# Router logits taken from transposed, un-normalised residual sums; second token tile's norm moved to ScalarE and GpSimd; weight splits moved beside the last expert

## The chip, the cores and the metric

The kernel runs on one core of one Trainium2 chip. The metric is device time in microseconds. Three runs of the kernel before gave a median of 1345.87 us (1345.45 to 1346.3). About 0.2% (2.7 us) is what a measurement of this kernel can tell from no change.

## The reference, cut to what matters

256 tokens of width 1024 pass two layers of a first block and one layer of a second block. In each of the first two layers a mixer (retention in layer 0, sparse attention "nsa" in layer 1) is followed by a layer norm, a mixture of 16 experts and another layer norm:

```python
h = layer_norm(ALPHA * h + mix, ln_mix_g[l], ln_mix_b[l])
h = layer_norm(ALPHA * h + moe(h, router_w, router_b, gate[l], up[l], down[l]), ln_ffn_g[l], ln_ffn_b[l])

# moe: x is the normed h
aff = sigmoid(x @ router_w)                 # 16 scores a token
sel = aff + router_b                        # best group of 4, then the best 2 experts in it
w = aff * chosen; w = w / w.sum(-1)
for e in range(16):
    y += w[:, e:e+1] * ((silu(x @ w_gate[e]) * (x @ w_up[e])) @ w_down[e])
```

With s the residual sum before the norm, mu its mean and r its inverse deviation, the logits of the normed x are r * (s @ (g * W)) - r * mu * sum(g * W) + sum(b * W); g and b are the norm's gain and shift, W the router's weights.

## The kernel before, in words

Each engine has its own instruction stream, written out in the order in which it runs: PE (TensorE), DVE (VectorE), ACT (ScalarE), POOL (GpSimd), and SP (SyncE), which issues nearly all transfers in order on one queue. They meet only at semaphores. Tokens come in two tiles of 128, `tt` = 0 and 1. `X` holds the residual stream, tokens on partitions.

Dense linears: weights come in blocks of 512 x 512 f32 (1 MB) into a ring `raw` of 7. ACT copies a block to fp32r `whi` (`split_hi`, L489), DVE subtracts to `wlo` (`split_lo`, L499), PE multiplies three products. Two blocks (`AHEAD`) of the next linear are split ahead of it. Activations are split likewise: PE transposes `X` (L742), ACT writes `th` (L749), DVE writes `tl` (L757).

Around a router (`out_and_norm_*`, L1062 on, then `moe_layer_*`, L2715 on): PE makes the output linear tile by tile (L615). DVE adds ALPHA * X + product (`residual_half`, L1051), takes statistics, and norms `X` in place (`centre_half` L810, `shift_half` L814), with the root on ACT. Only then PE transposes the normed tile, ACT and DVE split it, PE makes the logits (L1103, L1108), DVE reduces them (L1140), ACT takes the sigmoid (L1131), and DVE ranks experts in some 40 small instructions up to L1183. PE meanwhile puts ALPHA * X into PSUM with 8 matmuls on `ident_a` (L1113), counted by `rows_summed`. Then come slot numbers (L1122 to L1127), one-hot `pick` tiles (L1212), and the gather of each expert's tokens from `xn_h`/`xn_l`, the split copy of `X` (L1379).

Experts (`paired_*`, L1310 on): 96 blocks of 1 MB go through 20 homes. Sixteen homes come free before or during the output linear and are filled early. Home 16 (`rows`) is the memory of `X` itself: SP waits at L1323/L1324 for `xn_l_done` and `rows_summed` before it issues, and all later issues of the queue stand behind it. Every later block waits for the use of the block 20 before it. After block 95 SP issues the two rows of the next norm (`gb`, L1342), and then the next linear's `raw` blocks. For the last expert, 15, the order on ACT is: transposed hidden (L1502), `y(14)` (L1495), `y(15)`, then the two `split_hi` of the next linear (L2743), then the table of the root (L2744). DVE makes the low half of `y` (L1539) behind ACT's, PE scatters it to the rows (L1442), and DVE norms tile 0, then tile 1 (L3084 on). The two `split_lo` stand between: before the low half of the transposed tile 0, and behind tile 1's norm.

Of the kernel before, what the change touches and what calls it, by code (L numbers as in the profile page):

```python
# [53 lines left out]
C_ID, C_ROW, C_BEFORE, C_ONES, C_COL, C_I16, C_I4, C_FOLD, C_END = 0, 128, 448, 576, 580, 584, 600, 604, 668  # L54
# [45 lines left out]
def block_program(nc, a, out):  # L100
    with ExitStack() as ctx:
# [41 lines left out]
        ident_a, pre_gT = small[:, 128:256], small[:, 64:64 + DC]  # L143
        rw = keep("rw", [P, DC, E], F32)
# [4 lines left out]
        class Arena:  # L149
# [15 lines left out]
        fold = cst[:, C_FOLD:C_FOLD + SLOTS]  # L165
# [12 lines left out]
        ang = A("ang", [P, 4, TT, 96], at=gb_at + 4096 + 1024)  # L178
        ret_sd = A("ret_sd", [P, 2, 3, P], at=gb_at)
# [130 lines left out]
        cmp_loaded, cmp_turned, cmp_copied, cmp_built = (  # L310
            sem(n) for n in ("cmp_loaded", "cmp_turned", "cmp_copied", "cmp_built"))
# [13 lines left out]
        x_late, conv_loaded, conv_turned, conv_taken = (  # L325
            sem(n) for n in ("x_late", "conv_loaded", "conv_turned", "conv_taken"))
# [101 lines left out]
        halved = [l_ret_out, l_nsa_out, l_b_out, l_mix, l_down]  # L428
        two_piece = [l_up.b0 + 20, l_up.b0 + 21]
# [78 lines left out]
        def linear_sync(sp, l, between=None):  # L508

            def body(j, turn):  # L510
                for kb, kc in enumerate(l.groups):
                    if between is not None:
# [549 lines left out]
        def out_and_norm_tensor(pe, l, xh, xl, layer, c0=0, opened=False, low=same, ready=None):  # L1062

            def first_half(tt, n):
                if tt == 1 and n == 1:
                    half_turn_tensor(pe, 1 + 2 * layer, tokens(X), normed_by(pe, 4 * layer), (0,))
            halves_tensor(pe, l, xh, xl, in_order, c0, opened, None, first_half, low, ready)

        def out_and_norm_scalar(act, l, layer):
# [3 lines left out]
            early_table(ACT.Sqrt)  # L1073
            root_half(act, 4 * layer, 0)
            half_turn_scalar(act, 1 + 2 * layer, 0)
            nc.scalar.activation(straight(xn_h, 0), neighbours(X, 0), ACT.Copy).then_inc(xn_h_done, 1)
            root_half(act, 4 * layer, 1)

        def out_and_norm_vector(dve, st, o, l, layer):

            for i in (2, 3):
                split_lo(dve, sweep_first, l.b0 + i, 0)
            residual_half(dve, o, l, 0, 0)
# [9 lines left out]
        def router_tensor_logits(pe, k, layer):  # L1093
            for tt in range(TT):
                if tt == 1:
                    half_turn_tensor(pe, k, tokens(X), normed_by(pe, 4 * layer), (1,))
                at = 2 * E * tt
                if tt == 0:
                    pe.wait_ge(half_lo, 4 * k + 2)
                for half in range(2):  # L1100
                    pe.wait_ge(half_hi, 4 * k + 2 * tt + half + 1)
                    for c in range(4 * half, 4 * half + 4):
                        nc.tensor.matmul(PS[:, 4, at:at + 2 * E], th[:, c, tt * P:(tt + 1) * P],  # L1103
                                         rwx[:, c].rearrange("p a e -> p (a e)"), start=(c == 0), stop=False,
                                         skip_group_check=True)
                    pe.wait_ge(half_lo, 4 * k + 2 * tt + half + 1)
                    for c in range(4 * half, 4 * half + 4):
                        last = nc.tensor.matmul(PS[:, 4, at:at + E], tl[:, c, tt * P:(tt + 1) * P], rwx[:, c, 0, :],  # L1108
                                                start=False, stop=(c == DC - 1), skip_group_check=True)
            last.then_inc(to_vector, 1)  # L1110
            for tt in range(TT):
                for half in range(2):
                    last = nc.tensor.matmul(PS[:, 2 * tt + half, :], ident_a[:, :], X[:, tt, half * BW:(half + 1) * BW],  # L1113
                                            start=True, stop=False, skip_group_check=True)
            last.then_inc(rows_summed, 1)

        def router_tensor(pe, st, k, layer):

            router_tensor_logits(pe, k, layer)
# [9 lines left out]
        def router_scalar(act, st):  # L1129
            inbox(act, st)  # L1130
            nc.scalar.activation(affinity, score, ACT.Sigmoid).then_inc(to_vector, 1)  # L1131
# [353 lines left out]
        def paired_scalar(act, s, layer):  # L1485
# [22 lines left out]
            for e in range(E):  # L1508
# [8 lines left out]
                if e >= 1:  # L1517
                    y(e - 1)
# [1819 lines left out]
```

## Time and profile before

| | us |
|---|---|
| median of three runs | 1345.87 |
| the profiled execution, its own time | 1347.77 |
| its span (first to last instruction) | 1345.6 |
| PE busy | 1279.1 (95%) |
| DVE busy | 737.5 (55%) |
| ACT busy | 539.2 (40%) |
| GpSimd busy | 74.9 (6%) |
| queue of SP (q1), share of 16 transfer engines | 66.0% |

The span is what the engines' instructions cover; 2.2 us of the execution lie outside it. The busy share of PE is an average over stages: it says nothing of a stage in which PE waits for DVE or for a transfer. A stage is read from the instructions in order of time and from what ended their idle time.

### The profile page before, as it was taken

Reading aid. Unit: us, or ns where it says so; the run is one execution under the profiler, and the core shown is the slowest. Engines: PE = TensorE matmul, PEld = TensorE weight load, DVE = VectorE, ACT = ScalarE, POOL = GpSimd, SP = SyncE. Lnnn points to the kernel's source line nnn. Section 1 sums busy time; section 2 is a strip of 40 time slices with the busy share of each in tenths; the row PEclk is TensorE's granted clock in tenths of the full one; section 3 lists DMA queues with packets and bytes.
Section 4 is the critical chain, followed back from the end, with each engine's and each line's share of the span. In section 5 each row is a group of like instructions: output and inputs, shape, how many; then the busy total and the mean of one; then the engine's idle time right before and its main releaser. Section 6 shows DMA issues by size and latency. Waiting matters only on the chain.

```text
span 1345.6 us, 16658 instructions
## 1 busy us (share of the span) xinstructions
PE 1279.1 (95%) x6652; PEld 893.4 (66%) x6652; DVE 737.5 (55%) x1231; ACT 539.2 (40%) x787; POOL 74.9 (6%) x78
## 2 busy tenths in 40 slices
PE   7999998999999799998999999799999998899998
PEld 5887887444443487676444443477888877899986
DVE  4766657233232685886233222675674566578772
ACT  4445442111121433682111111456546644465551
POOL 0000000000000000000000000006760000000000
PEclk9999998999999899898999999799999989899999
DMA  9654487999999655317999999664454426355540
GB/s 344 205 182 131 157 330 309 418 422 421 421 422 415 222 194 210 141 62 291 401 421 421 422 421 418 228 200 154 154 161 158 149 96 205 127 185 188 188 156 32
DMA packets 103890, 342.51 MB, mean 255 GB/s; under 512 B 10188, under 2 KB 17020, under 8 KB 79100
## 3 DMA queue, kind: packets, MB, share of 16 engines
q1 hardware_dynamic: 100992, 336.30, 66.0%
q10 hardware_dynamic: 2812, 5.04, 1.1%
q8 instruction: 57, 0.93, 0.3%
q14 instruction: 29, 0.24, 0.0%
HBM read 340.27 MB, written 1.05 MB: 254 GB/s over the span
## 4 chain that ended last, share of the span: by engine, by line
PE 87%; DVE 8%; ACT 3%; issue 1%; DMA 0%; ACTq 0%; DVEq 0%; SPq 0%
PE PS L690 23%; PE PS L1397 16%; PE PS L537 10%; PE PS L1431 9%; PE PS L615 7%; PE PS L593 5%; PE PS L674 2%; PE PS L1379 2%; PE PS L1442 2%; PE PS L742 1%; PE PS L2089 1%; DVE wlo L502 1%; PE PS L1816 1%; ACT whi L496 1%; PE PS L1842 1%
## 5 line engine op out<-in xcount | busy, mean ns | idle before, releaser
L502 DVE TENSOR_TENSOR wlo<-raw,whi 128x2048 fp32r<-128x2048 f32 (+1 forms) x122 | 272.7, 2255 | 101.7 <-ACT whi L496 97.2
L496 ACT ACTIVATE whi<-raw 128x2048 fp32r<-128x2048 f32 (+1 forms) x122 | 224.8, 1876 | 21.3 <-PE PS L593 13.9
L690 PE MATMUL PS<-whi,th 128*128 128x512 f32 x480 | 191.0, 398 | 1.6 <-ACT a_proj L2962 1.5
L690 PE MATMUL PS<-whi,tl 128*128 128x512 f32 x480 | 187.3, 390 | 0.0
L690 PE MATMUL PS<-wlo,th 128*128 128x512 f32 x480 | 186.9, 389 | 0.0
L1397 PE MATMUL PS<-moe_ring,xg 128*64 128x512 f32 x640 | 142.0, 593 | 2.6 <-DVE slot_sum L1555 2.6
L1397 PEld LDWEIGHTS PS<-moe_ring,xg 128*64 128x64 f32 x640 | 46.5, 137 | 91.6 <-issue 91.6
L1569 DVE TENSOR_TENSOR hidden<-hidden,PS 64x256 f32<-64x256 f32 x32 | 13.5, 423 | 170.0 <-ACT hidden L1512 170.0
L690 PEld LDWEIGHTS PS<-whi,th 128*128 128x128 f32 x480 | 90.2, 188 | 21.8 <-ACT a_proj L2962 1.9
L690 PEld LDWEIGHTS PS<-whi,tl 128*128 128x128 f32 x480 | 90.1, 188 | 19.1
L690 PEld LDWEIGHTS PS<-wlo,th 128*128 128x128 f32 x480 | 90.3, 188 | 17.6
L537 PE MATMUL PS<-th,whi 128*128 128x256 f32 x352 | 100.6, 286 | 1.4 <-DVE tl L757 1.4
L537 PE MATMUL PS<-th,wlo 128*128 128x256 f32 x352 | 100.4, 285 | 0.0
L537 PE MATMUL PS<-tl,whi 128*128 128x256 f32 x352 | 100.3, 285 | 0.0
L1539 DVE SCALAR_TENSOR_TENSOR y_split<-PS,w_slot,y_split 64x512 fp32r<-64x512 f32 x60 | 45.0, 749 | 93.7 <-ACT y_split L1495 92.8
L1512 ACT ACTIVATE hidden<-PS 64x512 f32<-64x512 f32 x32 | 18.9, 590 | 183.2 <-PE PS L1397 183.2
L1495 ACT ACTIVATE y_split<-PS,w_slot 64x512 fp32r<-64x512 f32 x60 | 40.9, 682 | 97.1 <-PE PS L1431 96.4
L1431 PE MATMUL PS<-moe_ring,hT 128*64 128x512 f32 x320 | 72.6, 598 | 0.0
L537 PEld LDWEIGHTS PS<-th,whi 128*128 128x128 f32 x352 | 68.4, 194 | 1.8 <-DVE tl L757 1.8
L537 PEld LDWEIGHTS PS<-th,wlo 128*128 128x128 f32 x352 | 68.4, 194 | 0.0
L537 PEld LDWEIGHTS PS<-tl,whi 128*128 128x128 f32 x352 | 68.4, 194 | 0.0
L879 POOL TENSOR_TENSOR rope_t<-b_proj,trig 128x256 f32<-128x256 f32 x48 | 41.5, 896 | 308.3 <-issue 295.3
(425 smaller groups left out, 2080.7 us busy)
## 6 DMA issues: line engine op xcount, KB each, us to landing
moe_ring<-in_moe_w_gate SPq DMA_DIRECT2D x40, 1024.0 KB, 14.1
moe_ring<-in_moe_w_up SPq DMA_DIRECT2D x40, 1024.0 KB, 16.2
moe_ring<-in_moe_w_down SPq DMA_DIRECT2D x40, 1024.0 KB, 19.8
raw<-in_w_in SPq DMA_DIRECT2D x32, 1024.0 KB, 5.2
raw<-in_ret_w_in SPq DMA_DIRECT2D x24, 1024.0 KB, 5.1
raw<-in_w_up SPq DMA_DIRECT2D x20, 1024.0 KB, 5.1
raw<-in_w_down SPq DMA_DIRECT2D x10, 1024.0 KB, 5.0
raw<-in_ret_w_out SPq DMA_DIRECT2D x8, 1024.0 KB, 4.9
```

The lines of the kernel that those rows point to most:

```text
L496: nc.scalar.activation(s.whi[:, high, 0:kc, 0:wide], s.raw[:, slot, 0:kc, 0:wide], ACT.Copy).then_inc(s.hi_done, 1)
L502: nc.vector.tensor_tensor(s.wlo[:, slot, 0:kc, 0:wide], s.raw[:, slot, 0:kc, 0:wide], s.whi[:, high, 0:kc, 0:wide], ALU.subtract).then_inc ...
L537: last = nc.tensor.matmul(PS[:, 2 * p + m // 2, (m % 2) * SEQ:(m % 2 + 1) * SEQ], w[:, k, c, m * P:(m + 1) * P], x[:, c0 + c, :],  start=( ...
L593: last = nc.tensor.matmul(PS[:, bank(j, tt), :], x[:, at, tt * P:(tt + 1) * P], w[:, k, c, :], start=(kb == 0 and c == 0 and i == 0), stop ...
L615: last = nc.tensor.matmul(PS[:, bank(j, tt), :], x[:, at, tt * P:(tt + 1) * P], w[:, k, c, :], start=(not opened and kb == 0 and c == 0 an ...
L674: last = nc.tensor.matmul(PS[:, 2 * (l.n0 % 2) + tt, :], x[:, KC * kb + c, tt * P:(tt + 1) * P], w[:, k, c, :], start=(kb == 0 and c == 0 ...
L690: last = nc.tensor.matmul(PS[:, 2 * (col % 2) + tt, 0:wide], x[:, KC * kb + c, tt * P:(tt + 1) * P], w[:, k, c, 0:wide], start=(kb == 0 an ...
L879: o(nc.gpsimd.tensor_tensor(t[i], u, v, ALU.mult))
L1397: m = nc.tensor.matmul(PS[64 * k:64 * k + 64, gate_up_bank(e), :], x, moe_place(layer, n)[:, c, :], start=(half == 0 and c == 0), stop=(ha ...
L1431: m = nc.tensor.matmul(PS[64 * half:64 * half + 64, down_bank_of(e), :], hT_of(e)[:, 2 * b + c, :], moe_place(layer, down_at(e) + b)[:, 2 ...
L1495: nc.scalar.activation(y_of(e)[rows, half, :], PS[rows, down_bank_of(e), :], ACT.Identity, scale=w_slot[rows, e:e + 1]).then_inc(s.y_hi, 1)
L1539: nc.vector.scalar_tensor_tensor(y_of(e)[low, half, :], PS[rows, down_bank_of(e), :], w_slot[rows, e:e + 1], y_of(e)[rows, half, :], ALU.m ...
```

## The change

What it does:

- Router: PE transposes the residual sums of a tile, not the normed rows, and multiplies them by `rwx`, now the split of g * W. `score_vector` (three DVE instructions a tile) applies mean and inverse deviation; the sigmoid takes scale -1. The constants sum(g*W), sum(b*W) of both layers are made once, during the first linear.
- `norm_half` of tile 0 waits on DVE for the transposes of its sums, because it writes over `X`.
- Tile 1 is normed by ACT (scale and bias) and GpSimd (gain, shift, two halves), GpSimd also makes half of its `xn_l`, DVE the other half, behind the first `pick`.
- Of the four ALPHA * X products of PE, one waits for tile 1's norm ahead of the slot-number matmuls, and the last, which counts `rows_summed`, stands behind the first four gathers.
- End of the experts: SP issues the next linear's first two blocks ahead of the norm's rows; ACT and DVE split them before `y(14)`; DVE takes tile 1's statistics ahead of the low half of tile 0; the next linear opens after the first half of tile 0.

```diff
         def opened_by(pe, k, turn=None):
             def opening(step):
                 if step == 0:
+                    pe.wait_ge(half_lo, 4 * k + 1)
+                if step == 1:
+                    if turn is not None:
+                        turn()
                     pe.wait_ge(half_lo, 4 * k + 2)
-                if step == 1 and turn is not None:
-                    turn()
...
+            def beside_out(tt, n):                      # out_and_norm_tensor
+                if tt == 1 and n == 0:
+                    for half in range(2):
+                        sums_turn_tensor(pe, l, 0, half)
+                if tt == 1 and n == 2:
+                    sums_turn_tensor(pe, l, 1, 0)
+                    for half in range(2):
+                        logits_tensor(pe, k, 0, half)
...
             root_half(act, 4 * layer, 0)                # out_and_norm_scalar
-            half_turn_scalar(act, 1 + 2 * layer, 0)
+            half_turn_scalar(act, k, 0)
+            act.wait_ge(normed, 4 * layer + 1)
             nc.scalar.activation(straight(xn_h, 0), neighbours(X, 0), ACT.Copy).then_inc(xn_h_done, 1)
+            half_turn_scalar(act, k, 1, (0,))
+            half_turn_scalar(act, k, 1, (1,))
             root_half(act, 4 * layer, 1)
...
             residual_half(dve, o, l, 0, 1)              # out_and_norm_vector
             dve.wait_ge(params_in, 16 * st.params)
+            dve.wait_ge(half_turned, 4 * k + 2)
             norm_half(dve, o, 4 * layer, 0)
             residual_half(dve, o, l, 1, 0)
-            half_turn_vector(dve, 1 + 2 * layer, 0)
+            half_turn_vector(dve, k, 0)
+            half_turn_vector(dve, k, 1, (0,))
+            inbox(dve, st)
+            score_vector(o, layer, 0)
             residual_half(dve, o, l, 1, 1)
-            norm_half(dve, o, 4 * layer, 1)
+            half_turn_vector(dve, k, 1, (1,))
+            dve.wait_ge(norm_root, RET_H + 4 * layer + 2)
+            o.then(nc.vector.reciprocal(small[:, 9:10], small[:, 9:10]))
+            o.then(nc.vector.scalar_tensor_tensor(small[:, 10:11], small[:, 2:3], -1.0, small[:, 9:10], ALU.mult,
+                                                  ALU.mult))
+            hand(dve, inverse_done)
...
+        def router_tensor(pe, st, l, layer):
+            k = 1 + 2 * layer
+            logits_tensor(pe, k, 1, 0)
+            sums_turn_tensor(pe, l, 1, 1)
+            logits_tensor(pe, k, 1, 1)
+            residual_tensor(pe, layer, 0, 0)
+            residual_tensor(pe, layer, 0, 1)
+            residual_tensor(pe, layer, 1, 0)            # each: pe.wait_ge(normed, 4 * layer + tt + 1), one matmul
             inbox(pe, st)
...
             selection(paired, 0, layer, rt2, 1)         # router_vector
+            dve.wait_ge(xn_h_done, 3 * layer + 3)
+            dve.wait_ge(xn_l_done, 3 * layer + 2)
+            nc.vector.tensor_tensor(straight(xn_l, 1)[:, 1], neighbours(X, 1)[:, 1], straight(xn_h, 1)[:, 1],
+                                    ALU.subtract).then_inc(xn_l_done, 1)
...
                 elif kind == "rows":                    # paired_sync
-                    sp.wait_ge(xn_l_done, 2 * (layer + 1))
+                    sp.wait_ge(xn_l_done, 3 * (layer + 1))
                     sp.wait_ge(rows_summed, layer + 1)
...
+            linear_sync(sp, behind_experts[layer], last=AHEAD)
             sp.wait_ge(moe_used, MOE_BLOCKS * layer + moe_last(moe_homes.index(("gains", 0))) + 1)
...
-            pe.wait_ge(xn_l_done, 2 * (layer + 1))      # paired_tensor
             for j in range(PER):
+                pe.wait_ge(xn_l_done, 3 * layer + 2 + j // 2)
                 if j == 3:
                     pe.wait_ge(s.xg_first, 2 * layer + 1)
                 gather(0, j, first_bank(j))
+            residual_tensor(pe, layer, 1, 1).then_inc(rows_summed, 1)
...
                 turned(e)                               # paired_scalar; paired_vector alike with split_lo
+                if e == E - 1:
+                    for b in range(AHEAD):
+                        split_hi(act, sweep_first, moe_b0[layer] + b, 0)
                 if e >= 1:
                     y(e - 1)
...
             early_table(ACT.Sigmoid)                    # moe_layer_scalar
-            half_turn_scalar(act, k, 1)
+            act.wait_ge(inverse_done, layer + 1)
+            act.wait_ge(half_turned, 4 * (1 + 2 * layer) + 4)
+            scaled_half(0)
+            router_scalar(act, st)
+            scaled_half(1)
             for h in range(2):
+                act.wait_ge(half_normed, 2 * layer + h + 1)
                 nc.scalar.activation(straight(xn_h, 1)[:, h], neighbours(X, 1)[:, h],
                                      ACT.Copy).then_inc(xn_h_done, 1)
-            router_scalar(act, st)
...
+                rows = [(slice(None), 1, slice(h * BW, (h + 1) * BW)) for h in range(2)]        # gpsimd
+                for h in range(2):
+                    pool.wait_ge(scaled_done, 2 * layer + h + 1)
+                    o.then(nc.gpsimd.tensor_tensor(X[rows[h]], X[rows[h]], gb[:, 0, h * BW:(h + 1) * BW], ALU.mult))
+                    nc.gpsimd.tensor_tensor(X[rows[h]], X[rows[h]], gb[:, 1, h * BW:(h + 1) * BW],
+                                            ALU.add).then_inc(half_normed, 1)
+                pool.wait_ge(half_normed, 2 * (layer + 1))
+                pool.drain().then_inc(normed, 1)
+                pool.wait_ge(xn_h_done, 3 * layer + 2)
+                nc.gpsimd.tensor_tensor(straight(xn_l, 1)[:, 0], neighbours(X, 1)[:, 0], straight(xn_h, 1)[:, 0],
+                                        ALU.subtract).then_inc(xn_l_done, 1)
...
             experts_norm_half(dve, o, 2, 0)             # behind the experts; alike in layer 1
-            split_lo(dve, sweep_first, l_nsa_kv.b0, 0)
+            experts_half(dve, st, o, 1, 0)
             half_turn_vector(dve, 2, 0)
-            experts_half(dve, st, o, 1, 0)
             experts_norm_half(dve, o, 2, 1)
-            split_lo(dve, sweep_first, l_nsa_kv.b0 + 1, 0)
```

In the first linear four transfers of 1024 single floats each (the norms' gains and shifts, one channel a partition) follow the other constants, DVE waits for them at its column 1 and makes four products of 128 x 128 there, and PE sums them over partitions with 8 matmuls of 64 columns behind block 4. Three more DVE instructions make layer 1's `rwx` after the experts of layer 0. The transfer semaphores of some tables are joined into fewer; the branch for crowded experts loads and splits the two blocks again.

## Rows read from the trace of the kernel before

**Rows 1.** Timeline, layer 0's router: start us, duration us, engine, instruction, [idle before, releaser].

```profile
213.97 0.51 PE L1103 MATMUL PS<-rwx,th 128*128 128x32 f32 x4
...
218.76 1.57 PE L742 MATMUL PS<-cst,X 128*128 128x128 f32 x8 [2.94 <-DVE X L814]
223.60 6.59 PE L1113 MATMUL PS<-X,small 128*128 128x512 f32 x8
224.51 0.19 DVE L1143 TENSOR_TENSOR route<-route,rb 128x32 f32<-128x32 f32 x1 [0.30 <-ACT route L1131]
229.19 0.38 DVE L1183 SCALAR_TENSOR_TENSOR picked_r<-route,tops 128x16 fp32r<-128x16 f32 x2
230.28 0.33 SPq L1336 DMA_DIRECT2D moe_rows<-in_moe_w_gate  x1
231.26 0.35 PE L1379 MATMUL PS<-pick,xn_h 128*128 128x256 f32 x1 [0.61 <-DVE pick L1212]
235.29 3.65 PE L1397 MATMUL PS<-moe_tail,xg 128*64 128x512 f32 x16
```

**Rows 2.** Windows: stretch, length, busy us by engine (instructions), granted clock, DMA share, GB/s.

```profile
226.00:230.30 4.30, 4.30 (x10) 1.81 (x8) 3.71 (x22) 0.00 (x0) 0.00 (x0) 0.60 0.08 32
240.00:300.00 60.00, 58.27 (x283) 25.02 (x281) 18.75 (x41) 10.33 (x18) 0.00 (x0) 1.00 1.01 420
...
365.00:409.00 44.00, 43.75 (x207) 17.50 (x204) 11.64 (x24) 7.33 (x13) 0.00 (x0) 1.00 1.01 422
```

**Rows 3.** GpSimd's groups by form: count, then busy us, mean ns of one.

```profile
L879 POOL TENSOR_TENSOR rope_t<-b_proj,trig 128x256 f32<-128x256 f32 x48 | 41.5, 896 | 308.3 <-issue 295.3 <-ACT b_proj L2962 12.2 <-POOL b_proj L882 0.3
...
L3019 POOL TENSOR_TENSOR xn_l<-X,xn_h 128x1024 fp32r<-128x1024 f32 x2 | 5.8, 2910 | 613.1 <-ACT xn_h L1076 613.1
```

**Rows 4.** SP's first `raw` issues at the end of both layers' experts, timeline.

```profile
417.77 23.21 SPq L486 DMA_DIRECT2D raw<-in_nsa_w_kv  x6
...
823.23 124.45 SPq L486 DMA_DIRECT2D raw<-in_w_in  x20
```

**Rows 5.** The first transfer of each: size, us from issue to landing.

```profile
raw<-in_nsa_w_kv SPq DMA_DIRECT2D x1, 1024.0 KB, 21.0
...
raw<-in_w_in SPq DMA_DIRECT2D x1, 1024.0 KB, 22.8
```

**Rows 6.** Timeline, end of layer 0's experts.

```profile
443.65 1.53 DVE L1539 SCALAR_TENSOR_TENSOR y_last<-PS,w_slot,y_last 64x512 fp32r<-64x512 f32 x2 [1.90 <-ACT y_last L1495]
444.35 3.71 ACT L496 ACTIVATE whi<-raw 128x2048 fp32r<-128x2048 f32 x2
445.32 1.16 PE L1442 MATMUL PS<-y_last,pickT 128*128 128x512 f32 x4 [1.32 <-DVE y_last L1539]
449.70 0.16 DVE L797 RECIPROCAL small<-small 128x1 f32<-128x1 f32 x1 [0.72 <-ACT small L793]
455.08 0.77 PE L674 MATMUL PS<-whi,th 128*128 128x512 f32 x1 [1.46 <-DVE tl L757]
461.45 0.50 PE L674 MATMUL PS<-whi,th 128*128 128x512 f32 x1 [1.08 <-DVE wlo L502]
```

**Rows 7.** Timeline, the same places in layer 1.

```profile
634.42 0.33 SPq L1336 DMA_DIRECT2D moe_rows<-in_moe_w_gate  x1
...
640.81 3.65 PE L1397 MATMUL PS<-moe_tail,xg 128*64 128x512 f32 x16
...
861.64 0.77 PE L674 MATMUL PS<-whi,th 128*128 128x512 f32 x1 [2.62 <-DVE tl L775]
```

**Rows 8.** Window of layer 1's first experts, columns as in rows 2.

```profile
645.00:700.00 55.00, 53.26 (x261) 23.32 (x259) 16.71 (x37) 8.58 (x15) 0.00 (x0) 1.00 1.00 409
```

**Rows 9.** The first linear: a transfer of 1024 single floats.

```profile
small<-in_pre_mix_g SPq DMA_DIRECT2D x1, 4.0 KB, 4.0
```

**Rows 10.** Timeline of DVE in the first linear.

```profile
43.37 4.49 DVE L502 TENSOR_TENSOR wlo<-raw,whi 128x2048 fp32r<-128x2048 f32 x2
48.56 1.43 DVE L865 TENSOR_TENSOR rope_t<-ret_proj,ret_c 128x256 f32<-128x256 f32 x4 [0.69 <-PE PS L690]
```

More of the change, by code:

```diff
@@ L506, in width_of, with linear_sync @@
             return max(at + wide for _, at, wide in l.sources(j, turn))
-        def linear_sync(sp, l, between=None):
+        def linear_sync(sp, l, between=None, first=0, last=9999):
             def body(j, turn):
                 for kb, kc in enumerate(l.groups):
+                    if not first <= len(l.groups) * j + kb < last:
+                        continue
                     if between is not None:
@@ new lines, in residual_tensor @@
+        def residual_tensor(pe, layer, tt, half):
+            pe.wait_ge(normed, 4 * layer + tt + 1)
+            return nc.tensor.matmul(PS[:, 2 * tt + half, :], ident_a[:, :], X[:, tt, half * BW:(half + 1) * BW],
+                                    start=True, stop=False, skip_group_check=True)
+        def router_tensor(pe, st, l, layer):
+            k = 1 + 2 * layer
+            logits_tensor(pe, k, 1, 0)
[4 more added lines that the diff above has]
+            residual_tensor(pe, layer, 1, 0)
@@ L1130, in router_scalar @@
             inbox(act, st)
-            nc.scalar.activation(affinity, score, ACT.Sigmoid).then_inc(to_vector, 1)
+            nc.scalar.activation(affinity, score, ACT.Sigmoid, scale=-1.0).then_inc(to_vector, 1)
         def router_vector(dve, st, o, layer):
@@ L1581, in paired_vector @@
                     crowded = crowded_of(dve, layer)
+                if e == E - 1:
+                    for b in range(AHEAD):
+                        split_lo(dve, sweep_first, moe_b0[layer] + b, 0)
                 if e >= 1:
@@ L2789, in moe_layer_sync @@
                 sp.wait_ge(sweep_second[layer].block_used, 2 * RING * E)
+                for n in range(AHEAD):
+                    (w, at, wide), = behind_experts[layer].sources(0, 0)
+                    sp.dma_start(raw[:, (moe_b0[layer] + n) % RAWS],
+                                 w[n * KC * P:(n + 1) * KC * P, :].rearrange("(c p) n -> p c n", p=P)).then_inc(
+                        sweep_second[layer].raw_ready[0], 16)
         block = ctx.enter_context(nc.Block())
@@ L2810, in first_rows, with beside_ret_in @@
                     pe.wait_ge(half_lo, 4)
-            steady_tensor(pe, l_ret_in, th, tl, lambda n: ret_beside_tensor(pe, n), first_rows)
+            def beside_ret_in(n):
+                if n == 4:
+                    inbox(pe, st)
+                    for c in range(DC):
+                        last = nc.tensor.matmul(PS[:, 7, 0:4 * E], cst[:, C_ONES:C_ONES + 1].broadcast_to([P, P]),
+                                                rw_gb[:, :, c, :], start=(c == 0), stop=(c == DC - 1))
+                    last.then_inc(to_vector, 1)
+                ret_beside_tensor(pe, n)
+            steady_tensor(pe, l_ret_in, th, tl, beside_ret_in, first_rows)
             def beside_open(n):
@@ L3242, in _ @@
             moe_layer_sync(sp, 1)
[L3243 removed]
+            linear_sync(sp, l_a_in, first=AHEAD)
+            for l in (l_b_in, l_gates, l_a_out, l_b_out, l_mix, l_up, l_down_open, l_down):
                 linear_sync(sp, l)
```

210 lines of the change are left out of this document (115 added, 95 removed).

## The prediction

> **What bounds the kernel now.** PE is busy 95% of the span, so I read the places where it isn't, in order of time: the timeline of the layers' routers, the timeline behind their experts, and then, since transfers share both places, the windows and SP's issues.
>
> In the router PE waits 2.9 us for the normed tile 1 (L742 at 218.76), and from the logits on everything hangs on DVE's ranking: sigmoid in at 224.51, last ranking instruction over at 229.57. The gather runs 231.26 to 235.29 and the first expert starts then [rows 1]. Layer 1 is the same, its first expert at 640.81 [rows 7]. Behind the experts PE waits for DVE twice (1.46 and 1.08 us end the idle times at 455.08 and 461.45) [rows 6].
>
> Between them is a second bound, which PE's busy share hides: all 16 transfer engines are full (share 1.01, 420 to 422 GB/s) from 240 to 300 and still from 365 to 409 [rows 2]. PE never waits there only because 16 blocks of 1 MB lie ready at the start. The stream of the other 80 starts with `moe_rows` at 230.28 [rows 1]; from 226 to 230.3 the engines rested (share 0.08) [rows 2]. So whatever delays that one issue delays all later landings, up to the next linear's weights.
>
> **The change, step by step (layer 0's times).**
>
> *PE before the router.* Four transposes and tile 0's 16 logit matmuls now stand ahead of the last output block: 0.5 + 4 x 0.5 [rows 1]; the output linear ends at 216.4 instead of 213.97. Tile 0's transposes only move.
>
> *Logits of tile 1.* Residual, statistics, the second half of the tile transposed and split, logits: ready at about 220.1; three score instructions of 0.2 each, sigmoid over at 221.4. Before: 224.5 [rows 1]. The ranking (5.1) is unchanged and ends at 226.5: 3.1 us gained.
>
> *Tile 1's norm on GpSimd.* ACT scales a half in 0.6; GpSimd starts at about 221.1, four 128 x 512 operations in a row. The trace has none of that size: 0.90 us for half of it and 2.91 for twice [rows 3]. Between them in proportion is 1.5; ends 0.9 and 2.9. 4 x 1.5 + 0.4 for waits: tile 1 is normed at 227.5 (ends 225.1 and 233.1).
>
> The Trainium skill (GPSIMD Engine Reference, "Elementwise — side-by-side cycle accounting") speaks against this step: two-input elementwise work costs GpSimd about twice VectorE's time, and it gives 4497 ns for 2048 elements; a quarter of that, an estimate, is 1.1 us, by which the sum would be some 1.5 us a layer smaller; no row here has the operation.
>
> *The new wait.* PE's third ALPHA * X product waits for that, and the slot-number matmuls queue behind it. At half clock a product takes 0.82 (6.59 / 8 [rows 1]): the slot matmuls start at 228.4, before 229.7. Of 3.1 us gained 1.3 is left. The first gather is at 230.2.
>
> *PE's clock.* It was granted 0.60 between 226 and 230.3 [rows 2], the lower level (1.2 GHz) for most of it, after 2.9 us of idle at 218.76; it came back while PE worked through eight products. Those stood where nothing waited for PE. Now PE is idle from about 221 to 227.5 and works next in the gather, on the path. The gather takes 4.0 us at full clock [rows 1], 8 at half. I take the level as back at 232: gather over at 235.1, and the fourth product behind it, so the first expert starts at 235.6 (+0.3; ends -1.0 and +3).
>
> *The home in `X`.* `rows_summed` now comes from that fourth product, behind the gathers. `moe_rows` is issued at about 236.0 instead of 230.28: 5.7 us later (ends 4.2 and 8.5). The path loses almost nothing here, but the full stream of transfers moves by all of it. In layer 1: 640.81 + 0.3 + 0.4 against 634.42 is 7.1; its stream has gaps, 409 of 421 GB/s over 55 us [rows 8], which give back 1.6: 5.5 us.
>
> *Splits beside expert 15.* ACT must have both `raw` blocks before `y(14)`. The first landed at 417.77 + 21.0 = 438.8 [rows 4, 5], behind 1 MB of norm rows; now the blocks go first, so the second lands where the first did. With 5.7: 444.5. Then ACT's split 1.9 (3.71 / 2 [rows 6]), DVE's split 2.25 (4.49 / 2 [rows 10]), DVE's low halves of y(14) and y(15), 2 x 1.53 [rows 6]: scatter at 451.7 to 451.8. Before: 445.32 [rows 6]. 6.4 us lost; 0.7 would be with no later stream. In the old order the blocks could land as late as 444.35 at no cost; that cover is gone. The experts' own last blocks move by the same 5.7; I cost them nothing apart from this, since PE then waits for the same chain. Layer 1: the first block landed at 823.23 + 22.8 = 846.0 [rows 4, 5], which is 1.7 later beside its first expert's 405.5 us; of that I take half: 5.5 + 0.7 + 0.9 = 7.1 us lost.
>
> *Behind the experts.* Root table without the splits in front: 0.7 of DVE's wait goes (0.72 at 449.70). First product needs half a tile: 0.9 more (455.08 to 453.5). Without `split_lo` of the second block (1.08 of waiting at 461.45), and with tile 1 normed by 457.2, its transposes follow the first 12 products: the second block starts at 458.75 instead of 461.45 [rows 6]. 2.7 us gained. In layer 1 the transposes are not what is late; the gain at 861.64 [rows 7] is 0.7 + 1.1 = 1.8.
>
> *First linear.* PE is full there; 8 small matmuls of 0.13 to 0.4 each: +1.1 (1 to 3). DVE works 1.3 more ahead of 43.37, so of the two splits there the first ends at 46.9 instead of 45.6; PE begins that block when it ends the one before, at about 48.5, which frees DVE's rotation at 48.56 [rows 10]: hidden, with 1.6 to spare. Four transfers of single floats, 4.0 us from issue to landing for the one shown [rows 9], delay the constants and the blocks behind them by 2 to 6; that is hidden or costs 2 at most. Layer 1's `rwx` and the joined semaphores: nothing, DVE is idle there.
>
> **Sum.** Layer 0: +6.4 - 2.7 = +3.7. Layer 1: +7.1 - 1.8 = +5.3. Start +1.1. Total +10.1. The profiled execution took 1347.77 us, of which 2.2 lie outside its span of 1345.6; it would become 1357.9. It stood 1.9 above the median, so the median becomes 1345.87 + 10.1 = 1356.0.
>
> **Rivals.**
>
> 1. *The gain arrives (the other side).* Mechanism: the stream of transfers gives the delay back between `moe_rows` and block 95, so both `raw` blocks are there when ACT comes to them (438.2 and before). It decides if the delay at the last blocks is under about 1 us. Then the layers give 2.7 + 1.8, lose 0.7 twice, and, if the clock is kept and GpSimd is quick, start their experts 1.5 earlier each; less 1.1: 5.0 us faster, 1340.9. For it: every issue but `moe_rows` waits for PE, not for that. Against: share 1.01 for the whole length [rows 2]. 14%.
> 2. *Gain and loss cancel.* Half of the delay is given back, or GpSimd at 1.1 us with the clock kept (delay 4.2) and landings early: 2 to 3 us a layer less, and up to the bound of 2.7. 1343.2 to 1348.6. 11%.
> 3. *The norm on GpSimd is the bound.* It shares the memory with DVE's ranking; at 2 us or more an operation tile 1 is normed at 229.6 or later and PE's gather runs all at 1.2 GHz: delay 8.5 in both layers, and PE waits for blocks as well. 10.1 + 2 x 2.8 = 15.7: 1361.6. For it: GpSimd's 0.90 for only 256 columns. Against: 2.91 for 1024. 12%.
> 4. My forecast, 1349 to 1360: 63%.
>
> That is slower by over 0.2% (2.7 us, what a measurement can tell) 75%, within it 11%, faster 14%. The range for 8 in 10 leaves out most of rival 1 and half of rival 3: 1345 to 1361.
>
> **What would show it.** Right: `moe_rows` issued 5 us or more later beside the first expert's start; no gap in the stream's share; ACT idle before the first split beside expert 15, released by a transfer; the last scatter 5 to 8 us later against the first expert; half clock in the gather; DVE's ranking about 3 us earlier; PE released by GpSimd's drain before the slot matmuls. Wrong: `moe_rows` at its old place, ACT's splits without a wait, or the second and third linears opening more than 3 us earlier. If the clock is full in the gather, each layer loses about 1.5 less.

## The result, and the profile after

The changed kernel takes 1362.4 us (median of 4 runs, 1361.4 to 1363.9), the kernel before in the same comparison 1345.7 (4 runs). The ratio is 1.0127, with a 95% interval of 1.0116 to 1.0139: slower by 16.7 us, where 10.1 were forecast. The profiled execution took 1363.87 us, its span 1362.1.

Laid side by side, the two timelines give the account. "Last scatter" is the start of `y_last`'s scatter, "second block" the opening on block 1 of the next linear ([rows 1, 6, 7] for before). Layer 1's router row runs from layer 0's second block and so holds the mixer between.

| part | measured, us | forecast, us |
|---|---|---|
| start, up to the router | +1.2 | +1.1 |
| router to first expert, layer 0 / layer 1 | +4.4 / +3.2 | +0.3 / +0.3 |
| first expert to last scatter | +6.0 / +6.1 | +6.1 / +6.8 |
| last scatter to second block | -0.8 / -2.4 | -2.7 / -1.8 |
| behind layer 1 | -1.2 | 0 |
| sum, of the profiled spans | +16.5 | +10.1 |

The measured column compares one profiled execution with one, and executions differ: layer 0's output linear starts at 191.29 in the kernel before and at 190.21 in e2, whose code up to there is the same. So a term of about 1 us isn't told from nothing; the router's 4.4 and 3.2 are.

So the late stream cost what was forecast, and the router is where it went wrong. The timeline of the changed kernel in layer 0's router, GpSimd and VectorE together (start us, duration us, engine, instruction, [idle before, releaser]):

```profile
221.94 0.21 ACT L1180 ACTIVATE route<-route 128x32 f32<-128x32 f32 x1
...
222.12 1.26 POOL L3112 TENSOR_TENSOR X<-X,gb 128x512 f32<-128x512 f32 x1 [7.13 <-ACT X L2801]
222.19 1.24 DVE L1191 TENSOR_TENSOR route<-route,rb 128x32 f32<-128x32 f32 x1 [0.32 <-ACT route L1180]
223.46 1.31 POOL L3113 TENSOR_TENSOR X<-X,gb 128x512 f32<-128x512 f32 x1
223.46 0.18 DVE L1198 TENSOR_TENSOR sums<-route 128x24 f32<-128x24 f32 x1
223.56 1.25 DVE L1199 TENSOR_TENSOR sums<-route 128x16 f32<-128x16 f32 x1
224.72 0.16 DVE L1200 TENSOR_TENSOR sums<-route 128x8 f32<-128x8 f32 x1
224.73 1.30 POOL L3112 TENSOR_TENSOR X<-X,gb 128x512 f32<-128x512 f32 x1
...
224.92 0.20 DVE L1201 TENSOR_REDUCE tops<-sums 128x2 f32<-128x48 f32 x1
...
227.50 2.08 PE L1157 MATMUL PS<-X,small 128*128 128x512 f32 x2 [4.58 <-POOLq L3116]
...
227.56 1.59 DVE L1212 TENSOR_TENSOR route<-route,pairs 128x16 f32<-128x16 f32 x2
...
232.11 0.38 PE L1171 MATMUL PS<-picked_r,before_r 128*128 128x16 f32 x1 [2.54 <-DVEq L443]
...
240.93 3.65 PE L1450 MATMUL PS<-moe_tail,xg 128*64 128x512 f32 x16
...
241.09 0.33 SPq L1388 DMA_DIRECT2D moe_rows<-in_moe_w_gate  x1
```

The sigmoid is in at 222.15, 2.3 us before [rows 1]. But L1191, which took 0.19 us before ([rows 1] have it as L1143), takes 1.24 and ends as GpSimd's operation ends; L1199 took 0.17 and takes 1.25. Not each one is held: L1198 and L1200, which also read two tensors in SBUF, start within 0.01 us of a GpSimd operation's start and take 0.18 and 0.16. The line of the kernel before for L1199:

```profile
224.84 0.17 DVE L1151 TENSOR_TENSOR sums<-route 128x16 f32<-128x16 f32 x1
```

The reduction at 224.92 reads one tensor and takes its 0.20 while GpSimd works. The ranking ends at 232.0, 9.8 us long instead of 5.1. PE had the normed tile at 227.5, as forecast, and then waited for the ranking. `moe_rows` is issued at 241.09, 10.8 later than before. Clock and stream (columns as in rows 2):

```profile
226.00:241.00 15.00, 10.55 (x43) 8.16 (x45) 11.81 (x44) 3.48 (x4) 2.83 (x3) 0.57 0.12 51
...
400.00:440.00 40.00, 39.24 (x176) 14.49 (x173) 9.79 (x21) 7.55 (x13) 0.00 (x0) 1.00 1.01 421
```

The gather runs at a granted clock of 0.57, and the transfer engines, nearly idle until `moe_rows` (share 0.12), are full from then on (1.01 from 245 to 446, and in the row shown). There (timeline, layer 0):

```profile
446.49 1.91 ACT L500 ACTIVATE whi<-raw 128x2048 fp32r<-128x2048 f32 x1 [4.56 <-DMA raw<-in_nsa_w_kv]
...
449.15 1.91 ACT L500 ACTIVATE whi<-raw 128x2048 fp32r<-128x2048 f32 x1 [0.75 <-DMA raw<-in_nsa_w_kv]
...
454.98 1.53 DVE L1596 SCALAR_TENSOR_TENSOR y_last<-PS,w_slot,y_last 64x512 fp32r<-64x512 f32 x2
...
456.94 1.91 PE L1495 MATMUL PS<-y_last,pickT 128*128 128x512 f32 x4
...
459.56 1.30 DVE L2844 BATCH_NORM_STATS2 small<-PS 128x6 f32<-128x512 f32 x2 [3.05 <-issue]
...
466.50 0.77 PE L682 MATMUL PS<-whi,th 128*128 128x512 f32 x1 [0.61 <-issue]
...
472.27 0.47 PE L682 MATMUL PS<-whi,th 128*128 128x512 f32 x1
```

ACT waits 4.56 and 0.75 us for the two blocks. The second is there at 449.15, 10.35 later than the 438.8 by which the forecast went. PE's last scatter is at half clock. VectorE's statistics then wait 3.05 us for nothing that the profile names ("issue"); before it was 0.7 us from scatter to statistics. Both are looked at below.

### The profile page after: what moved, and what is told of

Same layout as the page of the kernel before. It is cut to its first block, busy times and chain, and to the rows that moved or that the text cites. A ratio compares the mean times of both kernels' runs of the same rounds, so it can differ in the third digit from the quotient of the medians.

```text
span 1362.1 us, 16741 instructions
## 1 busy us (share of the span) xinstructions
PE 1281.9 (94%) x6668; PEld 894.2 (66%) x6668; DVE 745.5 (55%) x1245; ACT 541.8 (40%) x791; POOL 87.7 (6%) x88
## 4 chain that ended last, share of the span: by engine, by line
PE 84%; DVE 8%; DMA 4%; ACT 2%; issue 1%; ACTq 0%; DVEq 0%; SPq 0%
PE PS L698 23%; PE PS L1450 15%; PE PS L543 9%; PE PS L1484 7%; PE PS L621 7%; PE PS L599 5%; PE PS L682 2%; PE PS L1432 2%; PE PS L1495 2%; DMA raw<-in_w_in 2%; DMA raw<-in_nsa_w_kv 2%; DVE wlo L506 1%; PE PS L2149 1%; PE PS L1876 1%; PE PS L1902 1%
## 5 line engine op out<-in xcount | busy, mean ns | idle before, releaser
L887 POOL TENSOR_TENSOR rope_t<-b_proj,trig 128x256 f32<-128x256 f32 x48 | 45.3, 974 | 302.2 <-issue 288.8
```

The costliest lines, as they stand in the source:

```text
L887: o(nc.gpsimd.tensor_tensor(t[i], u, v, ALU.mult))
```

## The experiments

Medians of 4 or 10 runs; the ratio is to the kernel before, on the same chip. "Ranking" is its length and `moe_rows` its first issue, both in layer 0, "first expert" its start in layer 0 / layer 1, "gap" the idle time ahead of layer 0's statistics where no releaser is named.

| kernel | us | ratio, 95% | ranking | moe_rows | first expert | gap |
|---|---|---|---|---|---|---|
| after | 1362.4 | 1.0127 (1.0116-1.0139) | 9.8 | 241.1 | 240.9 / 654.8 | 3.1 |
| e1 router only | 1357.4 | 1.0080 (1.0063-1.0097) | 10.2 | 240.1 | 240.0 / 652.2 | 5.0 |
| e2 end only | 1346.1 | 1.0005 (0.9995-1.0016) | 5.1 | 229.1 | 234.6 / 640.2 | no |
| e3 narrow gain | 1355.8 | 1.0070 (1.0054-1.0087) | 6.3 | 236.8 | 236.6 / 647.0 | 3.1 |
| e4 rows early | 1351.9 | 1.0045 (1.0028-1.0062) | 9.8 | 234.1 | 238.4 / 647.4 | 3.6 |
| e5 e4, code moved | 1362.4 | 1.0125 (1.0107-1.0142) | 9.6 | 244.9 | 249.3 / 658.1 | no |
| e6 before, code moved | 1348.3 | 1.0014 (1.0004-1.0024) | 5.1 | 228.4 | 234.2 / 642.0 | 4.9 |
| e7 e4, PSUM ranking | 1348.8 | 1.0029 (1.0019-1.0039) | 5.2 | 233.9 | 238.1 / 644.4 | 3.1 |
| e8 e7, code moved | 1358.6 | 1.0100 (1.0080-1.0120) | 5.2 | 243.9 | 247.0 / 653.5 | no |
| e9 after, PE kept busy | 1362.4 | 1.0119 (1.0102-1.0136) | 9.9 | 239.9 | 239.7 / 653.4 | 3.1 |
| e10 e7, order, PE busy | 1346.0 | 0.9999 (0.9989-1.0008) | 5.2 | 230.6 | 233.7 / 638.3 | 3.0 |
| e11 e10, code moved | 1345.4 | 0.9995 (0.9985-1.0005) | 5.2 | 230.0 | 233.1 / 636.8 | no |
| e12 e11, old end | 1342.2 | 0.9977 (0.9966-0.9988) | 5.2 | 230.0 | 233.2 / 635.5 | no |
| e13 after, PSUM ranking | 1356.3 | 1.0086 (1.0069-1.0103) | 5.2 | 236.6 | 236.5 / 647.0 | 3.0 |
| e14 e13, code moved | 1356.0 | 1.0081 (1.0064-1.0098) | 5.2 | 238.1 | 237.9 / 647.4 | no |
| e15 e12, code not moved | 1345.1 | 1.0000 (0.9990-1.0010) | 5.2 | 230.9 | 234.1 / 639.0 | 5.0 |

**e1 and e2: the two halves of the change.** e1 is the changed kernel with the old end, e2 the kernel before with the new end. From e1's edit:

```
-            linear_sync(sp, behind_experts[layer], last=AHEAD)
...
-                if e == E - 1:
-                    for b in range(AHEAD):
-                        split_hi(act, sweep_first, moe_b0[layer] + b, 0)
...
+            for b in range(AHEAD):
+                split_hi(act, sweep_first, moe_b0[layer] + b, 0)
```

With these go DVE's `split_lo`, its order of work behind the experts and the opening's waits.

> The changed kernel with everything behind the experts as it was before: loads and splits of the next linear's two blocks behind the last y, statistics in the old order, opening on a whole tile. Theory (two losses that feed each other): the first expert still starts 5.6 us later in layer 0 and about 3 us more in layer 1, moe_rows is still issued near 241, but no ACT wait for a raw block stands ahead of the last two y, so of 16.7 us lost about 8.5 to 10 stay: 1354 to 1356 us. Rival (the late stream costs wherever its last blocks are split): 1361 to 1363 us.

Measured: 1357.4. With the old end ACT does not wait for `raw` ahead of the last `y`, and of 16.7 us 12.0 stay, more than the 8.5 to 10 expected; the 5.0 us gap ahead of the statistics was not in that sum. `moe_rows` is as late as in the changed kernel, yet from first expert to last scatter it is 210.0 us in both layers, as in the kernel before:

```profile
450.00 1.17 PE L1489 MATMUL PS<-y_last,pickT 128*128 128x512 f32 x4 [1.32 <-DVE y_last L1587]
```

So the late stream costs only through what ACT and DVE have queued behind the late blocks; with the old end it costs nothing.

> The kernel before with only the part behind the experts changed. Theory: moe_rows stays at 230.3, both raw blocks are there when ACT comes to them (438.8 and earlier), the last scatter is 0.7 us later and the two openings 2.7 and 1.8 us earlier: 1342 to 1344 us. Rival (two splits ahead of the last y are dear by themselves, whatever the stream does): the last scatter 4 us later or more in both layers, 1349 us or more.

Measured: 1346.1, no difference, where 1342 to 1344 was expected; neither theory was right. Timeline of e2, layer 0:

```profile
446.54 2.04 PE L1448 MATMUL PS<-y_last,pickT 128*128 128x512 f32 x4 [0.39 <-DVE y_last L1548]
...
452.80 1.97 PE L747 MATMUL PS<-cst,X 128*128 128x128 f32 x8 [4.22 <-DVE X L819]
...
455.37 0.77 PE L679 MATMUL PS<-whi,th 128*128 128x512 f32 x1 [0.61 <-issue]
...
460.30 1.03 PE L747 MATMUL PS<-cst,X 128*128 128x128 f32 x8
```

From first expert to last scatter it is 211.9 us against 210.0 before, so the splits ahead of `y` cost 1.9 (0.7 forecast), and the last scatter is slower (2.04 against 1.16). Nor were the two `raw` blocks there in time: ACT waits 0.84 and 0.66 us for them. From there to the second block (461.09) it is 14.55 against 16.13: 1.6 gained, not 2.7. The statistics start 1.2 us behind the slow scatter instead of 0.7, and the first product is 0.9 earlier instead of 1.6; then the opening's 12 products take 4.9 us instead of 4.3, ten of them at half clock (0.43 apart), where before seven were. These prices of the half clock were left out of that step.

**e3: GpSimd's part made narrow.**

```
-                rows = [(slice(None), 1, slice(h * BW, (h + 1) * BW)) for h in range(2)]
+                rows = [(slice(None), 1, slice(h * BW, h * BW + 16)) for h in range(2)]
```

> The changed kernel, where GpSimd's four gain and shift operations take 16 columns of each half instead of 512; the rest of the second tile's gain and shift is left out. Theory (GpSimd's operations hold up DVE's with two inputs in SBUF): the ranking takes 5.1 to 6.3 us instead of 9.8, its comparisons 0.2 us each again, moe_rows is issued 4 to 5 us earlier, 1352 to 1355 us. Rival (the ranking is longer by its new operands or places, not by GpSimd): ranking 9 us or more, 1361 to 1363 us.

Measured: 1355.8, 6.6 us less and just above the 1352 to 1355 expected. The timeline of e3 has the same instructions as above:

```profile
221.64 0.19 DVE L1191 TENSOR_TENSOR route<-route,rb 128x32 f32<-128x32 f32 x1 [0.32 <-ACT route L1180]
...
221.97 0.20 DVE L1199 TENSOR_TENSOR sums<-route 128x16 f32<-128x16 f32 x1
...
223.62 1.46 DVE L1212 TENSOR_TENSOR route<-route,pairs 128x16 f32<-128x16 f32 x2
```

Only L1212 is still long: it stands beside the one GpSimd operation that was left wide. The ranking is 6.3 us. `moe_rows` comes at 236.8, 4.3 earlier.

**e4: `moe_rows` issued early.**

```
             residual_tensor(pe, layer, 1, 0)
+            residual_tensor(pe, layer, 1, 1).then_inc(rows_summed, 1)
             inbox(pe, st)
...
-            residual_tensor(pe, layer, 1, 1).then_inc(rows_summed, 1)
```

> The changed kernel with the fourth ALPHA * X product directly behind the third, ahead of the wait for the ranking, as is rows_summed. Theory (the late stream is what ACT waits for beside expert 15): moe_rows is issued at about 235 instead of 241.1, the raw blocks land some 6 us earlier, ACT's waits of 4.6 and 0.7 us ahead of the splits go in both layers, 1351 to 1354 us. Rival (the landing beside expert 15 is set by the experts' own blocks and PE's use of them, not by moe_rows): ACT's waits stay, 1360 to 1363 us.

Measured: 1351.9, 10.5 us less. `moe_rows` goes at 234.1, ACT's waits shrink from 4.56 and 0.75 to 0.32 and 0.67 (layer 1: from 4.74 and 0.73 to 0.34 and 0.79), and from first expert to last scatter it is 4.6 us less in each layer. The first expert is 2.5 earlier too: 0.8 of it this execution had ahead of the router, the rest comes since the fourth product no longer stands behind the gather and the gather starts in full clock. Of what was varied this single line is the dearest.

**e5, e6: where VectorE's code lies.** In after the trace has a transfer of 8 KB on the DMA queue "instruction", 457.55 to 457.90. The transfer view of after for 457.5 to 458 (packets, MB, share of 16 engines):

```profile
DMA packets 93, 0.19 MB, mean 389 GB/s; under 512 B 1, under 2 KB 1, under 8 KB 92
## 3 DMA queue, kind: packets, MB, share of 16 engines
q1 hardware_dynamic: 92, 0.19, 102.2%
q14 instruction: 1, 0.01, 4.4%
```

The statistics start 1.66 us after its end. In e1, e3, e4, e6, e7, e9, e10, e13 and e15, the kernels with a gap, that distance is 1.65 to 1.66 us each time. In the kernel before two such transfers start at 446.76 and 448.29, when the statistics (446.06) have already begun. e5 and e6 move the code by instructions that do nothing (in e5 224 such lines, which build into 112 instructions, in e6 32 into 16):

```
+            for _ in range(224):
+                dve.wait_ge(x_in, 16)
             linear_side(dve, l_ret_open, split_lo)
```

> The kernel with the early fourth product (e4, 1351.9 us), and on VectorE 112 more instructions that only wait on a semaphore that was met long ago, ahead of the layer-0 linear, where VectorE idles. In e4 VectorE's statistics behind expert 15 of layer 0 start 3.5 us after its last y without a releaser, 1.65 us after an 8 KB transfer of the instruction queue ends; in layer 1 and in the kernel before they don't. Theory (the branch over the crowded case now lands in a piece of code that isn't loaded, and the load queues behind the full stream): the shift of the code puts the landing back into a loaded piece, the wait goes in layer 0, 1348.5 to 1350 us. Rival (VectorE waits for something of the schedule, PE or the queue): the gap of 3.5 us stays and the time is 1351.5 to 1352.5 us.

Measured: 1362.4, 10.5 more: a miss as a time. VectorE wasn't idle there, and PE waited 9.1 us for it. But the gap went: statistics at 462.37, 1.5 us behind the last `y` and released by PE, which gives back 2.0 of 11.1 us of delay. At layer 1's first expert the delay is 10.7 us again, so the gap's price can't be read from e5's time.

> The kernel before with 16 such waiting instructions on VectorE, as many as put its landing behind the branch where the changed kernel has it; nothing else is changed. Theory (place of the code): its statistics in layer 0 start 3 to 5 us behind the last y instead of 0.9, 1347.5 to 1350 us. Rival: no gap, 1344.5 to 1346.5 us.

Measured: 1348.3, 2.6 more. Timeline of e6, and the line of the kernel before for its last:

```profile
442.58 1.53 DVE L1539 SCALAR_TENSOR_TENSOR y_last<-PS,w_slot,y_last 64x512 fp32r<-64x512 f32 x2 [1.90 <-ACT y_last L1495]
...
449.03 1.30 DVE L2771 BATCH_NORM_STATS2 small<-PS 128x6 f32<-128x512 f32 x2 [4.92 <-issue]
```

```profile
446.06 1.29 DVE L2771 BATCH_NORM_STATS2 small<-PS 128x6 f32<-128x512 f32 x2 [0.88 <-PE PS L1442]
```

Sixteen idle instructions put the changed kernel's gap into the kernel before, 4.9 us of idle where 0.88 was. The code's place is the cause. That it acts by the load of the code behind the branch is argued, from the 1.65 us and from where the gap stands; the branch itself was not varied. The full stream during the load is there in every case with a gap, but it was not varied, so its share is open.

**e7, e8: one ranking input in PSUM.**

```
-        picked, slot_no, w_tok, score, rt1, rt2, rt3, affinity = (route[:, i] for i in range(8))
+        picked, slot_no, w_tok, score, _, rt2, rt3, _ = (route[:, i] for i in range(8))
+        in_bank = PS[:, 4, 128:128 + 4 * TT * E].rearrange("p (i t e) -> p i t e", i=4, t=TT)
+        rt1, rt2_p, affinity, score_p = (in_bank[:, i] for i in range(4))
...
-            o(nc.vector.tensor_tensor(sums[:, :, :, 0:3], s4[:, :, :, 0:3], s4[:, :, :, 1:4], ALU.add))
+            o(nc.vector.tensor_tensor(sums[:, :, :, 0:3], s4_p[:, :, :, 0:3], s4[:, :, :, 1:4], ALU.add))
```

> The kernel e4 with one input of each ranking operation of two in PSUM instead of SBUF (scores a second time, affinity, picks and pairs in a free part of bank 4; one more 128x32 operation). GpSimd's norm runs beside it as before. Theory (VectorE waits only where both inputs, or a fast copy form, use the SBUF port that GpSimd holds): the ranking takes 5.3 to 6.5 us instead of 9.8, e4's 1351.9 us falls by 3 to 4 us a layer, 1344 to 1347 us. Rival (any VectorE operation waits while GpSimd works in SBUF, or on this write side): 9 us or more, 1351 to 1353 us.

Measured: 1348.8, 3.1 us less than e4, where 1344 to 1347 was expected. Timeline of e7, the same stretch:

```profile
222.29 1.26 POOL L3117 TENSOR_TENSOR X<-X,gb 128x512 f32<-128x512 f32 x1 [7.13 <-ACT X L2806]
222.33 0.19 DVE L1195 TENSOR_TENSOR route<-PS,rb 128x32 f32<-128x32 f32 x1 [0.27 <-ACT PS L1184]
...
222.76 0.17 DVE L1205 TENSOR_TENSOR sums<-PS,route 128x16 f32<-128x16 f32 x1
...
227.59 3.78 PE L1160 MATMUL PS<-X,small 128*128 128x512 f32 x4 [4.50 <-POOLq L3121]
...
227.67 1.53 POOL L3123 TENSOR_TENSOR xn_l<-X,xn_h 128x512 fp32r<-128x512 f32 x1 [0.20 <-POOL X L3118]
...
228.32 0.93 DVE L1245 TENSOR_TENSOR route<-route,tops 128x32 f32<-128x32 f32 x1
...
232.66 0.55 PE L1438 MATMUL PS<-pick,xn_h 128*128 128x256 f32 x1 [0.41 <-DVE pick L1270]
```

GpSimd works just as long, and every operation with a PSUM input takes its old time; the one that still reads two SBUF tensors (L1245) is held, 0.93 for 0.19. The whole ranking is 5.2 us. The gain is less than the 4.6 saved a layer because PE's products at half clock now stand ahead of the slot matmuls.

> e7 and the 112 waiting instructions of e5 together. If both theories hold, the two add up: 1341.5 to 1344.5 us, below the kernel before. If the rankings' rival holds, as e5; if the rival on the code's place holds, as e7.

Measured: 1358.6, with e5's 9.1 us stall of PE in it again: a miss for the same reason.

**e9: PE kept busy in the changed kernel.**

```
-            residual_tensor(pe, layer, 0, 1)
+            for _ in range(5):
+                residual_tensor(pe, layer, 0, 1)
             residual_tensor(pe, layer, 1, 0)
+            for _ in range(2):
+                residual_tensor(pe, layer, 0, 1)
```

> The changed kernel with the second ALPHA * X product (of the first tokens) done four times more ahead of PE's wait for GpSimd and twice more ahead of its wait for the ranking; each time it gives the same sums. It keeps PE at work where it idles, nothing else moves. Theory (the gather's 6.2 us are half clock after idle time): the granted clock stays 1.0 from 222 to 240, the gather takes 4.0 us, first expert and moe_rows are 2 to 2.7 us earlier in each layer, 1357 to 1359 us. Rival (the gather waits for xg or the picks, the clock is beside it): 1361.5 to 1363 us.

Measured: 1362.4, no gain, and the clock did not stay. Windows of e9:

```profile
226.00:230.00 4.00, 4.00 (x10) 1.52 (x8) 3.80 (x11) 1.14 (x1) 2.55 (x2) 1.00 0.35 145
230.00:234.00 4.00, 1.62 (x11) 1.33 (x11) 3.55 (x17) 0.00 (x0) 0.00 (x0) 1.00 0.00 0
234.00:238.00 4.00, 4.00 (x24) 4.00 (x23) 3.28 (x15) 0.87 (x2) 0.00 (x0) 0.60 0.00 0
```

The gather begins at full clock, but PE was idle in most of 230 to 234, and the level falls in the gather itself (0.60 from 234 to 238). It took 5.4 us instead of 6.2. The first expert gained 1.2, which is less than a measurement of the whole can tell. What a gather wholly in full clock gives, e9 leaves open; e10 has one.

**e10 to e12: a version that beats both.**

```
-            residual_tensor(pe, layer, 0, 1)
-            residual_tensor(pe, layer, 1, 0)
-            residual_tensor(pe, layer, 1, 1).then_inc(rows_summed, 1)
+            for _ in range(5):
+                residual_tensor(pe, layer, 0, 1)
             inbox(pe, st)
...
+            residual_tensor(pe, layer, 1, 0)
+            residual_tensor(pe, layer, 1, 1).then_inc(rows_summed, 1)
```

What is left out between are the slot-number matmuls.

> e7 (early fourth product, ranking with one input in PSUM, 1348.8 us) with the products of the second tokens behind the slot-number matmuls instead of ahead of them, and the first tokens' second product done four times more in PE's idle time. In e7 the ranking ends at 227.6, but the slot matmuls wait behind four half-clock products until 230.4 and the gather starts at 232.7. Theory: slot matmuls at 227.8, gather at 230.3 and at full clock, first expert at 234.4 instead of 238.1, so 3 to 4 us less in each layer: 1341 to 1343.5 us, under the kernel before. Rival (the stream or the second tokens' low half holds the first expert): 1346 us or more.

Measured: 1346.0, 2.8 less than e7 and equal to the kernel before, where 1341 to 1343.5 was expected. The router came out as expected or better: gather at 229.35 with the clock at 1.00 (4.2 us from 229.3 to 233.5), first expert 233.7, `moe_rows` 230.6. The first experts are 4.3 and 6.0 us earlier than in e7, the end of the profiled execution 4.4; the medians differ by less, since e7's profiled execution stood 1.5 above its median. Where the rest goes is open.

> e10 and 112 instructions on VectorE that only wait on a semaphore long met, eight in each of the first 14 experts of layer 0, where VectorE idles 5 us each (in e5 the same number stood in one place and held PE up for 9.1 us, while the gap behind expert 15 went). Expected: the gap of 3.1 us without a releaser ahead of layer 0's statistics goes, 1.5 to 2.5 us less than e10: 1339 to 1342 us. If the waits delay the experts' own work instead, as much as e10 or more.

Measured: 1345.4, a miss (1339 to 1342 expected); the gap is gone, and the 0.6 us are not told from nothing.

> e11 with the loads, splits and statistics behind the experts as in the kernel before. If the part behind the experts is worth nothing by itself (e2: 1346.1 against 1345.4), within 1 us of e11; if it is worth 2 to 4 us once moe_rows is early, slower than e11 by that.

Measured: 1342.2, 3.2 less than e11 by the medians (two of its ten runs took 1346.3 and 1346.4) and 0.23% under the kernel before, little more than a measurement can tell, against the expectation that the new end is neutral or a gain. Timeline of e12:

```profile
233.15 3.65 PE L1451 MATMUL PS<-moe_tail,xg 128*64 128x512 f32 x16
...
443.69 1.17 PE L1496 MATMUL PS<-y_last,pickT 128*128 128x512 f32 x4 [1.31 <-DVE y_last L1593]
...
444.43 1.30 DVE L2828 BATCH_NORM_STATS2 small<-PS 128x6 f32<-128x512 f32 x2 [0.88 <-PE PS L1496]
...
459.79 0.50 PE L680 MATMUL PS<-whi,th 128*128 128x512 f32 x1
```

**e13 to e15: closing the account.** e13 is the changed kernel with e7's PSUM ranking alone, e14 adds eight idle instructions in each of the first 14 experts of layer 0, e15 is e12 without them.

> The changed kernel, in which each ranking operation reads one input from PSUM (as in e7) and nothing else differs: products, moe_rows and the end as in the change. This takes the one cost away that the forecast had at nothing, the ranking's 4.7 us, and keeps the late rows_summed. Theory: ranking 5.2 us, slot matmuls behind the third product at 228 to 229, moe_rows at 236.5 to 237.5 instead of 241.1, ACT's waits for the raw blocks still there, 1354 to 1356.5 us, where the forecast for the change was 1356.0. Rival (a large part of the 16.7 us is elsewhere): 1359 us or more.

Measured: 1356.3. `moe_rows` at 236.63 (236.0 forecast), ACT's waits still 4.41 and 0.78. That the time meets the forecast to 0.3 us is in part luck: the profiled execution's span is only 8.2 us over the kernel before's, the medians differ by 11.3, and the part behind layer 0's experts gained 0.9 instead of 2.7.

> e13 with the 112 waiting instructions of e11 spread over layer 0's experts. Theory (place of the code): the gap of 3 us ahead of layer 0's statistics shrinks to 1.5, 1 to 2.5 us less than e13. Rival: as e13.

Measured: 1356.0, less of a gain than the 1 to 2.5 us expected; the unnamed gap becomes 1.52 us behind PE, the time does not change measurably. Its profiled execution entered the experts 1.4 later than e13's, so the spans don't decide it either.

> e12 (1342.2 us) without its 112 waiting instructions. Theory: VectorE's statistics in layer 0 start 5 us behind the last y instead of 0.9, as in e1 and e6, and the time is 2.5 to 4 us more than e12: 1344.5 to 1346 us. Rival: within 1 us of e12.

Measured: 1345.1, 2.9 more than e12; the gap is 5.0. With the old end the place of the code is worth about 3 us, as in e6 (2.6); with the new end, where the scatter is later and the gap 3.0, it is under 1 (e11, e14).

## Why the prediction was wrong

- **"The ranking (5.1) is unchanged": the step that failed.** It is 9.8 us in layer 0 and 9.5 in layer 1. e3 and e7 show the cause: a VectorE operation with two SBUF inputs that comes while a GpSimd operation runs is held and ends with it. The forecast met this contention only as rival 3 and put it on GpSimd's side, 2 us or more an operation; GpSimd's took 1.26 to 1.31 us and lost 0.05 at most (the longer ones are those beside which L1198 or L1200 started), VectorE lost 4.7. The Trainium skill (SBUF — State Buffer, "SBUF: two separate sides") says it: the pair of ports shared by the two is an exclusive lock for a whole instruction, taken by VectorE in a two-port mode or with two SBUF inputs. The trace agrees; L1191's 1.24 us against 0.19 is the number.
- **What it cost.** 4.1 us at layer 0's first expert and 2.9 at layer 1's beyond the forecast, 7.0 in all. The end part is 1.9 and -0.6 off, the experts -0.1 and -0.7, the rest -1.2 and +0.1: 6.4 together, against 6.4 between the 16.5 of the spans and the 10.1. With the stall removed and nothing else (e13), the time is 1356.3, where 1356.0 was forecast (luck in part, as said at e13), and the way to the first expert is 0.6 us longer than before in layer 0 and the same in layer 1 (0.3 and 0.3 forecast).
- **The new wait for GpSimd's norm.** 227.5 forecast, 227.50 measured; 0.9 to 2.9 was the range of one operation, 1.5 the value taken, 1.3 what it was. It wasn't the bound in the changed kernel, the ranking was. In e7 it is.
- **`moe_rows` and the full stream.** Right in mechanism: no gap in the stream, both blocks later by what `moe_rows` was late, ACT waiting. 10.8 instead of 5.7, since it goes with the first expert; for the same reason the term from first expert to last scatter is right (6.0 and 6.1 for 6.1 and 6.8). e1 shows that it is paid only through the splits ahead of `y`; e4 takes 4.6 of it away in each layer, 10.5 us in all with what it gains in the routers.
- **PE's clock.** Half clock in the gather, as forecast; 6.2 us instead of 4.0, where 4.9 was forecast. (The forecast's first gather, 230.2, is 0.2 later than its own "1.3 is left" gives from 231.26.) PE had idled again before it (2.54 us ahead of the slot matmuls); in e10, where it had not, the gather took 4.2 us at clock 1.00.
- **Behind the experts.** -0.8 in layer 0 for -2.7. Half clock in the scatter and in ten of the 12 opening products (seven before), and the code's wait, were not in it; the first shows in e2, the second in e6. In layer 1 it was -2.4 for -1.8.
- **First linear.** +1.2 for +1.1, nearer than two executions can tell, since equal code differs by 1.1 us there.
- **The range** ended at 1361, 1.4 below the result, and left out half of rival 3. That rival's 1361.6 came close by luck: the right resource, with the stall on the wrong engine.

## What to carry to other kernels

Before moving elementwise work to GpSimd, look at what VectorE does in that stretch and count its operations with two SBUF inputs: each, however small, may wait for the whole of GpSimd's operation (1.24 us for 0.19 here), and one operand in PSUM avoided it (e7). A semaphore that releases a full stream of transfers is worth its own line in the sum: issue it before the work on the path, not behind it. Put a load's consumer in an in-order queue only where the load is early by more than any delay upstream.

## What the runs showed of the hardware that was not expected

- VectorE operations of 0.17 to 0.19 us took 1.24 to 1.25 beside GpSimd's of 1.26 to 1.31 us; with one input in PSUM 0.17 to 0.19. A `TENSOR_SCALAR` of 128x4 from SBUF to SBUF was held as well (two in 1.11 us instead of 0.36); from PSUM to PSUM in e7 it was not.
- VectorE can stand 3 to 5 us behind the branch over the crowded case, by all signs for the load of its code: 8 KB on the queue "instruction", with the start 1.65 to 1.66 us behind the transfer's end in ten kernels. Sixteen instructions more brought it (e6), 112 more took it away (e5, e8, e11, e12, e14).
- An instruction that only waits on a semaphore long met is not free: 112 in a row on VectorE ran from 176.62 to 187.58 in e5, 0.098 us each.
